# The first loads of a two-block kernel, moved between queues, with nine products ahead

## The reference

```
def swiglu(x, w_in, w_out):
    gu = x @ w_in
    return (jax.nn.silu(gu[..., :D_FF]) * gu[..., D_FF:]) @ w_out

h = jnp.concatenate([meta, x], axis=1)          # 272 x 1024
h = h + 0.5 * rmsnorm(swiglu(rmsnorm(h, gn[0]), ffn_w_in[i, 0], ffn_w_out[i, 0]), gn[1])
u = rmsnorm(h, gn[2])
y = mlstm_mixer(u, ...)
h = h + rmsnorm(y, gn[3])
h = h + 0.5 * rmsnorm(swiglu(rmsnorm(h, gn[4]), ...), gn[5])
```

## Time and profile before

| | |
|---|---|
| median of 3 runs | 1279.44 us (1276.63, 1279.44, 1282.45) |
| span of the profiled execution, first to last instruction | 1277.6 us |
| TensorE busy | 1242.6 us, 97% |
| VectorE, ScalarE, GpSimd busy | 910.9, 777.0, 249.2 us |
| mean granted TensorE clock | 0.991 of full |
| first product of the opening | 6.92 us |
| first product of unit 1 | 12.68 us |
| moved | 212.53 MB, 166 GB/s in the mean |

### The profile page before, as it was taken

The page is one execution under the profiler, slowest core; times in us unless marked ns, Lnnn a source line. Parts: engine busy times, 40 slices in busy tenths (PEclk is TensorE's granted clock), DMA queues, the critical chain, the costliest instruction groups (busy, mean ns, idle before and its releaser), DMA issues.

```text
span 1277.6 us, 28536 instructions
## 1 busy us (share of the span) xinstructions
PE 1242.6 (97%) x10472; PEld 1212.7 (95%) x10472; DVE 910.9 (71%) x1634; ACT 777.0 (61%) x1287; POOL 249.2 (20%) x226
## 2 busy tenths in 40 slices
PE   7999999999999999997999999999999999999997
PEld 7999999998999999995999989999999889999997
DVE  5866556887787665688877477777766697777654
ACT  5544445598564444567886696666665476666643
POOL 0000000010000000024576100245510231444400
PEclk9999999999999999998999999999999999999999
DMA  7655465464356556644757125765587524666463
GB/s 231 205 173 173 139 171 176 158 198 109 116 182 197 184 145 197 191 146 139 210 152 224 35 67 168 212 192 183 171 206 189 187 75 149 189 186 183 141 196 109
DMA packets 87804, 212.53 MB, mean 166 GB/s; under 512 B 19429, under 2 KB 34085, under 8 KB 87600
## 3 DMA queue, kind: packets, MB, share of 16 engines
q1 hardware_dynamic: 85504, 204.58, 53.1%
q0 software_dynamic: 1664, 6.48, 2.2%
q10 hardware_dynamic: 560, 0.44, 0.1%
HBM read 208.41 MB, written 3.06 MB: 166 GB/s over the span
## 4 chain that ended last, share of the span: by engine, by line
PE 89%; DVE 6%; ACT 2%; issue 1%; DMA 1%; DVEq 0%; ACTq 0%
PE bank L545 20%; PE bank L547 20%; PE bank L546 20%; PE bank L2857 3%; PE bank L2858 3%; PE bank L2859 3%; PE bank L1646 1%; PE bank L2983 1%; DVE wl L413 1%; PE bank L1648 1%; PE bank L1647 1%; PE bank L518 1%; PE bank L522 1%; PE bank L519 1%; PE bank L3494 1%
## 5 line engine op out<-in xcount | busy, mean ns | idle before, releaser
L408 ACT ACTIVATE wh<-raw 128x1024 fp32r<-128x1024 f32 (+3 forms) x423 | 407.4, 970 | 336.7 <-PE bank L547 286.5
L413 DVE TENSOR_TENSOR wl<-raw,wh 128x1024 fp32r<-128x1024 f32 (+3 forms) x364 | 402.6, 1110 | 146.7 <-ACT wh L408 145.8
L545 PE MATMUL bank<-XH,wh 128*128 128x256 f32 (+1 forms) x1448 | 411.5, 284 | 3.4 <-DVE XL L985 3.2
L547 PE MATMUL bank<-XH,wl 128*128 128x256 f32 (+1 forms) x1448 | 410.9, 284 | 0.0
L546 PE MATMUL bank<-XL,wh 128*128 128x256 f32 (+1 forms) x1448 | 410.6, 284 | 0.0
L545 PEld LDWEIGHTS bank<-XH,wh 128*128 128x128 f32 x1448 | 274.1, 189 | 4.4 <-DVE XL L985 3.6
L547 PEld LDWEIGHTS bank<-XH,wl 128*128 128x128 f32 x1448 | 274.4, 190 | 0.0
L546 PEld LDWEIGHTS bank<-XL,wh 128*128 128x128 f32 x1448 | 273.0, 189 | 0.0
L545 PE MATMUL bank<-AH,wh 128*128 128x256 f32 (+1 forms) x704 | 198.6, 282 | 0.0
L547 PE MATMUL bank<-AH,wl 128*128 128x256 f32 (+1 forms) x704 | 198.5, 282 | 0.0
L546 PE MATMUL bank<-AL,wh 128*128 128x256 f32 (+1 forms) x704 | 198.2, 282 | 0.0
(11 more groups left out here) (392 smaller groups left out, 2238.1 us busy)
## 6 DMA issues: line engine op xcount, KB each, us to landing
raw<-in_w_up SPq DMA_DIRECT2D x175, 512.0 KB, 4.3
raw<-in_w_down SPq DMA_DIRECT2D x64, 384.0 KB, 3.4
raw<-in_w_down SPq DMA_DIRECT2D x64, 320.0 KB, 3.2
raw<-in_w_gvz SPq DMA_DIRECT2D x32, 512.0 KB, 4.2
raw<-in_w_gout SPq DMA_DIRECT2D x16, 512.0 KB, 4.8
raw<-in_w_gqk SPq DMA_DIRECT2D x12, 512.0 KB, 4.0
raw<-in_w_mv SPq DMA_DIRECT2D x8, 512.0 KB, 4.5
raw<-in_w_mqk SPq DMA_DIRECT2D x8, 512.0 KB, 5.0
```

The source lines that it names most:

```text
L408: eng.activation(WH[s][:, 0:n, :], raw[s][:, 0:n, :], ACT.Copy).then_inc(s_hi[s], 1)
L413: eng.tensor_tensor(WL[s][:, 0:n, :], raw[s][:, 0:n, :], WH[s][:, 0:n, :].bitcast(F32), ALU.subtract).then_inc(s_lo[s], 1)
L545: eng.matmul(out, WH[s][:, i, :], xh, start=start, stop=False)
L547: mm = eng.matmul(out, WL[s][:, i, :], xh, start=False, stop=stop)
```

## The change

Five things change, all before or in the opening:

- The five loads of `H` leave SyncE's queue and stand on ScalarE's, behind `vec` and ahead of ScalarE's counting up. SyncE's queue begins with the weights.
- GpSimd holds the late vectors, constants and bias table back until the last weights of the opening (unit 3) have landed, instead of chunks 2 and 3 of `H`.
- VectorE writes `ones` first, with a semaphore of its own (`s_ones`), and `mean` ahead of its counting up.
- `s_ms` counts five tiles instead of six.
- TensorE, once `ones` is written, makes nine products of `ones` by `ones` (128 columns, fp32) into bank 0, which the first product of the opening overwrites.

```diff
@@ -49,7 +49,7 @@
 
 SLOTS = 4
 TILES = 8
-MEMSETS = 6
+MEMSETS = 5
 
 
 VEC = {}
@@ -305,7 +305,7 @@
         s_in, s_in2, s_cst = sem("s_in"), sem("s_in2"), sem("s_cst")
         s_first, s_first_hi, s_first_lo = sem("s_first"), sem("s_first_hi"), sem("s_first_lo")
         s_h0 = [sem(f"s_h0_{i}") for i in range(1 + DC // 2)]
-        s_ms = sem("s_ms")
+        s_ms, s_ones = sem("s_ms"), sem("s_ones")
         s_rel, s_bias = sem("s_rel"), sem("s_bias")
         s_bias_pe, s_bias_dve = sem("s_bias_pe"), sem("s_bias_dve")
 
@@ -3819,13 +3819,10 @@
 
         @block.sync
         def _(eng):
-            eng.dma_start(H[:, 0:1, :], a["h0"][:, 0:1, :]).then_inc(s_h0[DC // 2], 16)
             w0 = up1.weights[0].rearrange("p (g k) m -> p g k m", g=4)
             eng.dma_start(raw[0][:, 0:TILES:2, :], w0[:, :, 0, :]).then_inc(s_first, 16)
-            eng.dma_start(H[:, 1:2, :], a["h0"][:, 1:2, :]).then_inc(s_h0[0], 16)
             eng.dma_start(raw[0][:, 1:TILES:2, :], w0[:, :, 1, :]).then_inc(s_raw[0], 16)
             for u in range(1, SLOTS):
-                eng.dma_start(H[:, 2 * u:2 * u + 2, :], a["h0"][:, 2 * u:2 * u + 2, :]).then_inc(s_h0[u], 16)
                 load_opening(eng, up1, u)
             run_dma(eng)
             for c in range(0, DC - 4, 2):
@@ -3840,7 +3837,7 @@
             for s in LO_POOL:
                 eng.sem_inc(s_lo[s], 1)
             prime(eng, "pool")
-            eng.wait_ge(s_h0[1], 16)
+            eng.wait_ge(s_raw[SLOTS - 1], 16)
             eng.dma_start(vec[:, VEC["acw"]:VECS], a["vecs"][:, VEC["acw"]:VECS]).then_inc(s_in2, 16)
             eng.dma_start(cst[:, :], a["consts"]).then_inc(s_cst, 16)
             eng.dma_start(rel[0:BUCKETS, :], a["rel_table"]).then_inc(s_rel, 16)
@@ -3851,6 +3848,10 @@
         def _(eng):
             n = VEC["acw"]
             eng.dma_start(vec[:, 0:n], a["vecs"][:, 0:n]).then_inc(s_in, 16)
+            eng.dma_start(H[:, 0:1, :], a["h0"][:, 0:1, :]).then_inc(s_h0[DC // 2], 16)
+            eng.dma_start(H[:, 1:2, :], a["h0"][:, 1:2, :]).then_inc(s_h0[0], 16)
+            for u in range(1, SLOTS):
+                eng.dma_start(H[:, 2 * u:2 * u + 2, :], a["h0"][:, 2 * u:2 * u + 2, :]).then_inc(s_h0[u], 16)
             prime(eng, "act")
             eng.wait_ge(s_in, 16)
             eng.wait_ge(s_ms, MEMSETS)
@@ -3862,13 +3863,13 @@
 
         @block.vector
         def _(eng):
+            eng.memset(ones[:, :], 1.0).then_inc(s_ones, 1)
             for s in set(range(SLOTS)) - LO_POOL:
                 eng.sem_inc(s_lo[s], 1)
             eng.memset(scratch[:, :], EPS).then_inc(s_ms, 1)
+            eng.memset(mean[:, :], 1.0 / D).then_inc(s_ms, 1)
             prime(eng, "dve")
             eng.sem_inc(s_ev, 4)
-            eng.memset(ones[:, :], 1.0).then_inc(s_ms, 1)
-            eng.memset(mean[:, :], 1.0 / D).then_inc(s_ms, 1)
             for t in TP:
                 eng.memset(t[:, 0:3], 0.0).then_inc(s_ms, 1)
             eng.memset(rel[BUCKETS:BUCKETS + 1, :], NEG).then_inc(s_ms, 1)
@@ -3880,6 +3881,9 @@
             prime(eng, "pe")
             for s in range(SLOTS):
                 eng.sem_inc(s_pe[s], 1)
+            eng.wait_ge(s_ones, 1)
+            for _ in range(9):
+                eng.matmul(bank[0][:, 0:P], ones[:, :], ones[:, :], start=True, stop=True)
             eng.wait_ge(s_ms, MEMSETS)
             multiply(eng, up1)
             multiply(eng, down1, None, c_up1.rhs_wait(eng))
```

## The result

The changed kernel took 1281.64 us (median of 20 runs, 1279.19 to 1284.3), the kernel before 1278.22 (20 runs on the same chip, 1276.25 to 1282.81). The ratio is 1.0025, interval 1.0016 to 1.0035: 3.2 us more, between 2.0 and 4.5. The forecast was 1281.3, +1.9 on the profiled execution, and 1276.9 to 1284.3. The profiled spans are 1281.4 and 1277.6, +3.8.

What follows compares the result with a forecast made beforehand. TensorE, 97% busy, bounds the kernel, so only unit 1's start at 12.68 matters: unit 0 ending at 14.65, less 0.1, gives +1.9, span 1279.5; plus 1.84 for the median, 1281.3 (1276.9 to 1284.3).

Steps and rivals of the forecast that it cites:

- ScalarE's issues: Opening: five H loads and 25 increments ahead of the table load put it at 6.4, first product at 9.55, 2.6 later.
- The clock: Unit 0: low clock at the first product, rising 4.6 us after it (3.3 to 5.9), unit 0 ending at 14.65.
- the sum: Opening total: first product 9.55, low clock, unit 0 done at 14.65 against 12.68, less 0.1: +1.9 us.
- the gap at 586: TensorE's idle gap from 582.36, where the clock fell after 3.6 us; precedent for losing it after the dummies.
- The rival in which the clock holds: Opening: dummies raise the clock and the gap keeps it; unit 1 starts at 13.2 or 12.3, time 1279.4; chance 0.30.
- a first low-clock product of unit 1 before: Unit 1's start: 0.1 us subtracted from the loss, for a slow first product in the kernel before.
- the lower bound of the rise: Opening: shortest time to raise the clock, 3.3 us of dense products, read from the rise in 1002 to 1003.
- Unit 1's weights and the late constants: Opening: wl ready at 13.2, holding constants worth nothing; rival had H delay the weights, +1.4, 1280.8, chance 0.12.
- Issues one at a time: Opening rival: two queues take turns issuing, table load 8.85, first product 12.0, +4.5 less 0.1, 1283.8; chance 0.12.
- The failed step: After the opening: from unit 1 on, TensorE's intervals were expected unchanged, shifted by one constant, with no further loss.
- a new wait of TensorE after 15 us: Sign named beforehand: such a wait, or constants missing at 30, would make the prediction wrong in kind.

Runs made afterwards that it cites:

- Experiment 1: Kernel before with only the five loads of H moved to ScalarE's queue; ratio 1.0012 (1.0002 to 1.0022).
- 11: Changed kernel without the dummy products, ScalarE's 25 increments moved behind its four opening units; ratio 1.0009 (0.9998 to 1.0021).
- 8: Changed kernel again, unchanged, one execution for a second profile; first product that reads cst at 31.97 us (+1.94), last L632 4.75 behind.
- 5: Kernel before with only ones and mean written first and the nine dummy products; ratio 1.0021 (1.0011 to 1.0032).
- 6: Kernel before with ones and mean first, the nine dummy products, and ten more between unit 0 and unit 1; ratio 1.0017 (1.0005 to 1.0029).
- 4: Kernel before with only GpSimd's three late loads held back until unit 3's weights have landed; ratio 0.9998 (0.9988 to 1.0008).
- 10: Changed kernel with 36 semaphore increments on TensorE in place of the nine dummy products; ratio 1.0047 (1.0031 to 1.0063).
- 3: Kernel before with 59 more semaphore increments on ScalarE, no transfer moved; ratio 1.0029 (1.0016 to 1.0043).
- 2: Kernel before with 33 more semaphore increments on ScalarE, no transfer moved; ratio 1.0015 (1.0004 to 1.0025).
- 12: Kernel before with H's first two chunks on ScalarE, its increments late, and all memsets ahead of VectorE's increments; ratio 1.0008 (0.9997 to 1.002).
- 7: Changed kernel without its nine dummy products, the wait for ones kept; ratio 1.0008 (0.9996 to 1.002).

## Why the prediction was right, and where it was not

*ScalarE's issues, right.* Table load forecast 6.4, measured 6.31; first product 9.55 and 9.47. Experiment 1 gets all of it from this part alone, and 11 takes it away.

*The clock: the level right, the way to it not.* Unit 0 ran at the low level. The rise came 4.9 us behind the first product, where the sum had 4.6. Unit 1: 14.65 forecast, 14.74 measured; the opening +1.9 and +1.95. But the sum gave the idle time behind the products (3.41 us) as the reason for the low level, as in the gap at 586, and that was not put to the test: the products had not raised the clock when they ended, and the first rise on record is at 14.35 (14.26 in 8). That the forecast chose the low level for a reason that did not come into play is luck. The same products at the same time had the clock up at 5.15 in 5 and at 6.11 in 6; why not in the change is open, and what a gap of 3.4 us would have done to a raised clock is not shown. The rival in which the clock holds fell here for want of a rise; in 5, with 1.0 us of idle time behind the products, the level was kept. Its price for the kernel (gain bounded by unit 1's `wl`) was right as well: 6 reached -0.64.

*Two readings behind these numbers were off.* The 0.1 for "a first low-clock product of unit 1 before" is there, but that product was at the high level: the clock had risen at 12.60, and its weight load took 0.19, where in 5, at the low level, it took 0.29. Its step of 0.23 is what a first product behind a wait takes at the high level in 4, too (clock up at 11.16). And the lower bound of the rise, 3.3 us at 999, is counted from the fall of the clock; TensorE had been at work since 997.40, 5.1 us.

*Unit 1's weights and the late constants, right.* `wh` of unit 1 did not wait, and 4 shows the constants worth nothing.

*Issues one at a time, refuted.* The five loads on ScalarE took 0.45 and 0.52, then three in 2.04, with SyncE's 0.68, 0.61 and three in 1.97 beside them; before, on one queue, 0.41 to 0.70 each. The Trainium skill, Perfetto Trace Analysis, section DMA Instruction — HWDGE (DVE, Sync), says that the descriptor generator is locked for one sequencer at a time. At these durations no such turn-taking shows: ten issues ended at 4.26, where a single queue needed until 6.37. A lock that takes up only a part of each issue would not be seen here.

*The failed step* is in the last sentence of the prediction, "from unit 1 on every interval of TensorE as before, shifted by one constant". The term for it was zero. It measured +0.3 by 694 us, 0.8 at L2946 (1.82 in the second execution) and 0.75 behind that. By the prediction's own words "a new wait of TensorE after 15 us" makes it wrong in kind, and there is one. The dummy products were priced by what they do in the opening alone. They also lengthened TensorE's instruction stream, and with as many increments in their place the wait stays (10). It comes some 680 us after them.

How much of the median's +3.2 (2.0 to 4.5) is the wait can't be told exactly. The opening's 1.95 leaves about 1.3, and with the products taken out the difference is 1.0 (-0.5 to 2.6), but 3 was timed 3.7 slower (2.0 to 5.5) with +2.32 at the marker and no wait at L2946. The forecast of 1281.3 also started from a median of 1279.44, where the larger set gave 1278.22; the predicted time came out as close as it did because the two errors, 1.2 too much there and 1.3 too little in the change, nearly cancel, and that is luck.

*Left open.* Timed and traced differences don't agree in 2 (+1.9 timed, +0.3 by 722 us in the trace), in 3 (+3.7 and +2.9), in 10 (+6.0 and +2.9) and in 12 (+1.0 and about 0). Six to twelve runs whose own scatter is 5 us don't settle it, and other packets may meet other transfers in executions that were not profiled.

## What to carry to other kernels

Before a transfer's issue is moved to an engine that computes, count everything that then stands between it and that engine's first useful instruction; here 3.5 us of issues and 25 increments (1.8 us) behind them made the start 2.5 us late, and moving the increments away took the opening's loss back. A clock raised early can be lost in the next wait (in 5, idle for 1.0 us kept it and 2.34 lost it), so first ask what TensorE waits for next; and see in the trace whether the products raised it at all. And a difference can start far from the edit: here 36 more instructions on the busiest engine brought a wait some 680 us later, with instruction packets shifted against tight transfers as the likely carrier. Where a kernel runs at its bound, look for such differences there.

## What the runs showed that was not expected

*The clock near 1000 us makes much of the span's scatter.* In every kernel TensorE waits at L545 there. In before the clock then falls; in 10 and 12, whose waits were 0.80 us, it doesn't:

```profile
999.00:1000.00 1.00, 0.89 (x6) 0.68 (x6) 0.66 (x2) 1.00 (x3) 0.00 (x0) 1.00 0.86 311
1000.00:1001.00 1.00, 1.00 (x10) 1.00 (x11) 0.91 (x1) 1.00 (x3) 0.00 (x0) 1.00 0.36 143
```

That is 10. It gains 2.9 us on the kernel before between 722 and 1003 us, and 12 gains the same. In 4 and 5 it did not fall either, after waits of 1.78 and 2.14; in the others it fell after 1.26 to 2.85, for some 3 to 4 us (before, 1, 2, 7, 11 and after's second execution) or 6 and more (after, 3, 6). The length of the wait alone doesn't decide. In after, the longer stretch is part of the last 0.75 us. No part of the change was seen to cause it, and a single profile's span carries up to 3 us of it either way. 2, 4 and 5 have 1.21 us of waiting at L3529 near 1045 us that the other eleven profiles don't have, which is not explained either.

*The clock rose between 3.3 and 5.7 us after TensorE's first product* at the low level: 3.3 in 11, 3.4 in 3, 3.9 in 10, 4.2 to 4.3 in 2, 4 and 12, 4.9 in 1, 7 and after (4.8 in 8), 5.7 in both executions of before. Behind the first dummy product it rose after 3.3 in 5 and 4.2 in 6, and in after and 8 not in the 4.2 us that the products lasted.

*The PEclk column reads 1.00 in the opening* even where four products of L522 take 1.11 us, so there the level has to be read from the products' durations.
